# A two-layer hybrid decoder step: the sample tile of the mLSTM taken second, the second prompt tile last

## What is computed

```python
b = jnp.cumsum(lfc, axis=-1)
dmat = jnp.where(causal, b[..., :, None] - b[..., None, :] + lic[..., None, :], -jnp.inf)
inter = b + m[..., None]
m_t = jnp.maximum(inter, dmat.max(-1))
g_inter = jnp.exp(inter - m_t)
s = jnp.einsum('bhtd,bhsd->bhts', qc, kc) * jnp.exp(dmat - m_t[..., None])
num = g_inter[..., None] * jnp.einsum('bhtd,bhde->bhte', qc, C) + jnp.einsum('bhts,bhse->bhte', s, vc)
den = g_inter * jnp.einsum('bhtd,bhd->bht', qc, n) + s.sum(-1)
h = num / jnp.maximum(jnp.abs(den), jnp.exp(-m_t))[..., None]
...
C = dec[..., None, None] * C + jnp.einsum('bhs,bhsd,bhse->bhde', ws, kc, vc)
```

## Time and profile before

| what | us |
|---|---|
| median of 3 runs (lowest, highest) | 1525.32 (1524.56, 1529.46) |
| the profiled execution | 1525.5 |
| its span | 1523.7 |
| PE busy in the span | 1470.8 (97%) |
| DVE, ACT, POOL busy | 983.7, 696.0, 378.4 |
| growth multiply of step 14, 18, 26 starts, layer 0 | 420.86, 433.85, 456.96 |

### The profile page before, as it was taken

The page is one execution under the profiler, slowest core; times in us unless marked ns, Lnnn a source line. Parts: engine busy times, 40 slices in busy tenths (PEclk is TensorE's granted clock), DMA queues, the critical chain, the costliest instruction groups (busy, mean ns, idle before and its releaser), DMA issues.

```text
span 1523.7 us, 34030 instructions
## 1 busy us (share of the span) xinstructions
PE 1470.8 (97%) x13394; PEld 1415.6 (93%) x13394; DVE 983.7 (65%) x1579; ACT 696.0 (46%) x1188; POOL 378.4 (25%) x407
## 2 busy tenths in 40 slices
PE   7999999999988999999999999989999899999995
PEld 7999998899867999999999999979998689999995
DVE  4444435588475787775577776466874777877644
ACT  5333334766545543334443334366574455333332
POOL 4222362010531422220412222300124313222100
PEclk9999999999999999999999999999999999999998
DMA  8544543444113655544544545534521444555351
GB/s 220 151 145 146 166 152 83 132 121 122 33 40 112 172 152 151 151 138 152 158 132 144 151 152 157 151 90 124 131 74 31 122 116 138 160 151 170 126 166 35
DMA packets 318938, 198.82 MB, mean 130 GB/s; under 512 B 7792, under 2 KB 303760, under 8 KB 318832
## 3 DMA queue, kind: packets, MB, share of 16 engines
q1 hardware_dynamic: 315120, 190.69, 43.0%
q0 software_dynamic: 3712, 6.62, 2.2%
HBM read 188.50 MB, written 8.78 MB: 129 GB/s over the span
## 4 chain that ended last, share of the span: by engine, by line
PE 85%; DVE 8%; ACT 4%; issue 2%; DVEq 1%; DMA 0%; SPq 0%; ACTq 0%
PE bank L2113 24%; PE bank L2115 23%; PE bank L2114 23%; DVE wlo L2606 2%; PE bank L2200 1%; ACT whi L2403 1%; DVE raw L1571 1%; DVE rlo L2637 1%; PE bank L747 1%; ACT z L1176 1%; PE bank L2205 1%; PE bank L777 1%; PE bank L571 1%; PE bank L848 1%; PE bank L759 1%
## 5 line engine op out<-in xcount | busy, mean ns | idle before, releaser
L2403 ACT ACTIVATE whi<-raw 128x1024 fp32r<-128x1024 f32 x340 | 358.0, 1059 | 471.9 <-PE bank L2115 455.6
L2606 DVE TENSOR_TENSOR wlo<-raw,whi 128x1024 fp32r<-128x1024 f32 x340 | 421.4, 1243 | 228.7 <-ACT whi L2403 227.9
L2113 PE MATMUL bank<-rhi,whi 128*128 128x322 f32 x984 | 306.5, 311 | 0.0
L2115 PE MATMUL bank<-rhi,wlo 128*128 128x322 f32 x984 | 305.9, 311 | 0.0
L2114 PE MATMUL bank<-rlo,whi 128*128 128x322 f32 x984 | 304.9, 310 | 0.0
L2113 PE MATMUL bank<-xh,whi 128*128 128x320 f32 x912 | 284.9, 312 | 5.2 <-DVE xl L2780 3.2
L2114 PE MATMUL bank<-xl,whi 128*128 128x320 f32 x912 | 281.8, 309 | 0.0
L2115 PE MATMUL bank<-xh,wlo 128*128 128x320 f32 x912 | 281.8, 309 | 0.0
L2875 POOL TENSOR_TENSOR hl<-scratch,hh 128x320 f32 x88 | 146.9, 1669 | 494.9 <-DVE scratch L2727 379.6
L2113 PE MATMUL bank<-hh,whi 128*128 128x320 f32 (+1 forms) x704 | 218.4, 310 | 0.5 <-DVE wlo L2606 0.5
L2114 PE MATMUL bank<-hl,whi 128*128 128x320 f32 (+1 forms) x704 | 217.4, 309 | 0.0
(11 more groups left out here) (421 smaller groups left out, 1908.9 us busy)
## 6 DMA issues: line engine op xcount, KB each, us to landing
raw<-in_ffn_wg SPq DMA_DIRECT2D x88, 512.0 KB, 3.8
raw<-in_ffn_wu SPq DMA_DIRECT2D x88, 512.0 KB, 3.8
raw<-in_ffn_wd SPq DMA_DIRECT2D x88, 512.0 KB, 3.6
raw<-in_w_in SPq DMA_DIRECT2D x60, 512.0 KB, 3.8
raw<-in_w_out SPq DMA_DIRECT2D x16, 512.0 KB, 6.1
raw<-in_state_C SPq DMA_DIRECT2D x8, 512.0 KB, 6.1
out_s_C<-raw SPq DMA_DIRECT2D x8, 512.0 KB, 4.1
ring<-in_state_wkv POOLq DMA_DIRECT2D x8, 256.0 KB, 5.9
```

What stands on the lines that cost most here:

```text
L2113: pe.matmul(out, w_hi, hi, start=start, stop=False)
L2115: return pe.matmul(out, w_lo, hi, start=False, stop=stop)
L2403: act.activation(whi[:, slot, :], raw[:, slot, :], ACT.Copy).then_inc(hi_ready.sem, 1)
L2606: dve.tensor_tensor(wlo[:, slot, :], raw[:, slot, :], whi[:, slot, :].bitcast(F32), ALU.subtract).then_inc(lo_ready.sem, 1)
```

## The change

The sample becomes the second of the three tiles in time (`TURN`), and prompt tile 1 the last. The scores of the sample are now at step 9, its heads at steps 12 and 13, its C pieces at steps 14 to 17, two a step, its means, squares and spreads at steps 15 and 16. Prompt tile 1 has its scores at step 18, values at 21, memory added and means at 22, spreads at 23, scaling at 24, output products at 25. ACT's load of the table for the square root moves behind step 19. The exponential of the gate row goes to a buffer of its own for the sample (`rexp_s`).

`tile_scores` no longer spreads rows with `sel`. It transposes a column of `cols`, broadcast along the free axis. For this `gate_columns` turns five rows (four for tile 0), 14 products in place of 9, and `cols` has five columns.

On POOL the first `masked_values` goes to the front, `decay` waits only for the columns, and the first `memory_term` waits for the prompt's spreads (`hvar_ready` 2).

```diff
@@ gate_columns
-                for q in range(3):
-                    last = turn(pe, bank[4][0:rows, (n * 3 + q) * HB:(n * 3 + q + 1) * HB], row[:, q, at:at + rows])
+                for i, r in enumerate(COLUMNS):
+                    if n or i < 4:
+                        out = (n * 5 + i) * HB
+                        last = turn(pe, bank[4][0:rows, out:out + HB], row[:, r, at:at + rows])
@@ tile_scores
-                pe.wait_ge(num_ready.sem, num_ready.by(L, n))
-                pe.wait_ge(caug_ready.sem, caug_ready.by(L, n))
-            for r, b in ((5, 4), (6, 5)):
-                if n or r == 5:
+                pe.wait_ge(num_ready.sem, num_ready.by(L, TURN[n]))
+                pe.wait_ge(caug_ready.sem, caug_ready.by(L, 1))
+                if n == 1:
+                    pe.wait_ge(left_done.sem, left_done.by(L, 2 * HB))
+            for i, b in ((3, 4), (4, 5)):
+                if n or i == 3:
                     for h in range(HB):
-                        pe.matmul(bank[b][:, h * rows:(h + 1) * rows], sel[:, h, :], row[:, r, at:at + rows],
-                                  start=True, stop=True)
+                        pe.transpose(bank[b][:, h * rows:(h + 1) * rows],
+                                     cols[0:rows, n, i, h:h + 1].broadcast_to([rows, P]), ident[0:rows, 0:rows])
...
+        TURN = (0, 2, 1)
@@ tensor_mixers
-                    tile_scores(pe, L, 1 + SCORES_AT.index(n))
+                    tile_scores(pe, L, TURN[1 + SCORES_AT.index(n)])
...
-        LEFT = (("C", 0), ("C", 1), ("C", 2), ("C", 3), ("H", 0), ("H", 1), ("C", 4), ("C", 5), ("C", 6), ("C", 7),
-                ("H", 2), ("N", 0), ("T", 0))
+        LEFT = (*(("C", i) for i in range(2 * HB)), ("H", 2), ("H", 0), ("H", 1), ("N", 0), ("T", 0))
...
-        NUM_AT = (7, 12)
-        SCORES_AT = (9, 14)
-        HEAD_AT = (17, 18)
-        LEFT_AT = (20, 20, 21, 21, 22, 22, 23, 23, 24, 24, 25, 26, NSTEP)
+        NUM_AT = (7, 21)
+        SCORES_AT = (9, 18)
+        HEAD_AT = (12, 13)
+        LEFT_AT = (14, 14, 15, 15, 16, 16, 17, 17, 23, 25, 25, 26, NSTEP)
@@ scalar_mixers
-                if n == SQUARES_AT[0]:
+                if n == WEIGHTS_AT[2] + 1:
                     act.preload_act_table_set("sqrt_and_others")
...
-        WEIGHTS_AT = (4, 9, 14)
-        NUMS_OUT_AT = (7, 12, 19)
-        SQUARES_AT = (17, 20)
-        ROOTS_AT = (19, 22)
+        WEIGHTS_AT = (4, 9, 18)
+        NUMS_OUT_AT = (7, 13, 21)
+        SQUARES_AT = (15, 22)
+        ROOTS_AT = (20, 23)
@@ vector_mixers
-        LOGS_AT = (10, 15)
-        PRODUCTS_AT = (6, 11, 16)
-        ADDED_AT = (8, 13)
-        QUERIES_AT = 17
-        INTER_AT = 17
-        MEANS_AT = (17, 20)
-        SPREADS_AT = (19, 21)
-        SCALED_AT = (20, 23)
+        LOGS_AT = (10, 19)
+        PRODUCTS_AT = (6, 11, 20)
+        ADDED_AT = (8, 22)
+        QUERIES_AT = 12
+        INTER_AT = 13
+        MEANS_AT = (15, 22)
+        SPREADS_AT = (16, 23)
+        SCALED_AT = (21, 24)
@@ pool_mixers
+            masked_values(pool, L, 0)
             pool.memset(qm[:, :, :], 0.0).then_inc(qm_zero.sem, 1)
...
-            pool.wait_ge(tile_mm.sem, tile_mm.by(L, NTT))
+            pool.wait_ge(cols_turned.sem, cols_turned.by(L, 1))
...
-            pool.wait_ge(hvar_ready.sem, hvar_ready.by(L, 1))
+            pool.wait_ge(hvar_ready.sem, hvar_ready.by(L, 2))
             memory_term(pool, L, 1)
```

More of the change, by code:

```diff
@@ L195, in hymba_kernel @@
         gnst = area(3888, 2, NCH * NJ)
-        lim = area(3928, 32, rows=HB)
-        cols = area(3960, NTT, 3, HB)
-        small = area(4008, 96)
+        lim = area(3928, 24, rows=HB)
+        cols = area(3952, NTT, 5, HB)
+        small = area(4012, 88)
         n0 = area(4104, SB, HB)
@@ L259, in hymba_kernel @@
         hsq = area(0, 2 * HB * DK, of=spare)
-        vmask = [area(1536, SB, DK, of=spare), area(15304, SB, DK)]
+        vmask = [area(9480, SB, DK), area(15304, SB, DK)]
         s0 = area(12744, SB, NJ, NA)
@@ L516, in bonus_sums @@
             last.then_inc(rk_mm.sem, 1)
+        COLUMNS = (1, 2, 0, 5, 6)
         def gate_columns(pe, L):
@@ L645, in left_over @@
             elif kind == "H":
-                pe.wait_ge(h_ready.sem, h_ready.by(L, 1 if i < 2 else 2))
+                pe.wait_ge(h_ready.sem, h_ready.by(L, 2 if i < 2 else 1))
+                if i == 2:
+                    pe.wait_ge(caug_ready.sem, caug_ready.by(L, 2))
                 rows = TT[i][1]
@@ L1058, in copy_gate_columns @@
                 rows = TT[n][1]
-                src = bank[4][0:rows, n * 3 * HB:(n + 1) * 3 * HB].rearrange("p (q h) -> p q h", q=3)
-                act.activation(cols[0:rows, n, 0, :], src[:, 0, :], ACT.Copy)
-                last = act.activation(cols[0:rows, n, 1:3, :], src[:, 1:3, :], ACT.Exp)
-            last = act.activation(cols[PART[1], 2, 2, 0:HB:2], bank[4][PART[1], 8 * HB:9 * HB:2], ACT.Exp)
+                src = bank[4][0:rows, n * 5 * HB:(n + 1) * 5 * HB].rearrange("p (q h) -> p q h", q=5)
+                kept = 5 if n else 4
+                act.activation(cols[0:rows, n, 0:2, :], src[:, 0:2, :], ACT.Exp)
+                act.activation(cols[0:rows, n, 2:kept, :], src[:, 2:kept, :], ACT.Copy)
+            own = (2 * 5 + 1) * HB
+            last = act.activation(cols[PART[1], 2, 1, 0:HB:2], bank[4][PART[1], own:own + HB:2], ACT.Exp)
             last.then_inc(cols_ready.sem, 1)
@@ L1105, in tile_weights @@
             rows = TT[n][1]
-            act.wait_ge(tile_mm.sem, tile_mm.by(L, n + 1))
+            act.wait_ge(tile_mm.sem, tile_mm.by(L, TURN[n] + 1))
             if n:
-                act.activation(rexp[:, 0:HB * rows], bank[5][:, 0:HB * rows], ACT.Exp)
-            act.wait_ge(wlog_ready.sem, wlog_ready.by(L, n + 1))
+                act.activation((rexp if n == 1 else rexp_s)[:, 0:HB * rows], bank[5][:, 0:HB * rows], ACT.Exp)
+            act.wait_ge(wlog_ready.sem, wlog_ready.by(L, TURN[n] + 1))
             act.activation(wexp[0:rows, :, 0:rows], wexp[0:rows, :, 0:rows], ACT.Exp).then_inc(wexp_ready.sem, 1)
@@ L1570, in left_over_done @@
                     at = h * TS + s * ST + ST - 1
-                    last = dve.scalar_tensor_tensor(out=C0[:, h, s, :], in0=C0[:, h, s, :], scalar=rexp[:, at:at + 1],
+                    last = dve.scalar_tensor_tensor(out=C0[:, h, s, :], in0=C0[:, h, s, :], scalar=rexp_s[:, at:at + 1],
                                                     in1=b[:, k * DK:(k + 1) * DK], op0=ALU.mult, op1=ALU.add)
```

77 lines of the change are left out of this document (40 added, 37 removed).

## The result

The changed kernel takes 1544.69 us (median of 4 runs, 1544.19 to 1545.47), the kernel before 1525.04 beside it: a ratio of 1.0121, 95% interval 1.0106 to 1.0136. It is 1.2% slower, and above the range that was forecast, 1521 to 1535. The span of the profiled execution went from 1523.7 to 1543.1 us, by 19.4.

What follows compares the result with a forecast made beforehand. PE was taken to bound steps 5 to 14, DVE steps 18 to 26; per layer 0.9 - 2.5 + 2.5 + 2.8 = +3.7, for two +7.4, less 4.4 gives +3.0: 1528.3 us, range 1521 to 1535.

Steps and rivals of the forecast that it cites:

- the sum: Whole kernel: +3.7 us per layer, +7.4 for two, less 4.4, gives +3.0; forecast chance 0.48.
- steps 5 to 14: Growth front, bound by PE: sample replaces tile 1, -2.5 us per layer (-1.2 to -3.6); DVE's masked queries cost nothing.
- the clock: Slow stretch in front, 1.7 us: taken away there, none added in the tail, its gain left out of the -2.5.
- the recurrence: Stage behind the growth: both PE waits without a releaser go, -4.4 us for both layers; 0 if kept.
- PE's late instructions: Recurrence: PE's waits of 2.7 and 1.7 us, laid to w_out loads, vanish as these are issued inside the growth: -4.4.
- the tail runs at the lower clock: Rival, steps 18 to 26: one more slow stretch per layer gives 1531.7 us, two more 1535.1; chance 0.17.
- The gate columns: Ahead of step 5, PE-bound: five more turns cost +0.9 us per layer, bounds 0.6 and 1.1.
- Steps 14 to 18: Now bound by DVE with eight memory updates and a 2.3 us first wait: 15.5 us, +2.5 per layer (0 to +3.5).
- Steps 18 to 26: Tail, a chain of single pieces of the last tile: 25.9 us in place of 23.1, +2.8 per layer (0 to +5).
- the scaling beside POOL: Tail: DVE's scaling runs beside POOL's `memory_term`, 1.0 us added in steps 18 to 26.
- the tail is relieved: Rival: steps 18 to 26 stay at 23.1 us as DVE loses its updates; 1520.5 us, faster; chance 0.18.
- The rule on transposes: Skill's statement that transposes don't count as PE-busy the same way; by it they would bring slow stretches; left undecided.

Runs made afterwards that it cites:

- tuned: The changed kernel with POOL's decay behind the second masked values, memory terms waiting for the scaled outputs, five added PE products of 384 columns: 1531.78 us, ratio 1.0033.
- decay late: The changed kernel with POOL's `decay` put behind the second masked values: 1542.08 us, ratio to the kernel before 1.0098.

## Why the prediction was wrong

The forecast was 1528.3 us, with slower by more than 0.3% at 0.40, and the sign of the sum (+3.0) was right; its size was not. Two steps failed: a term that was put at nothing in steps 5 to 14, and the clock, which the sum held at its level of before, in the recurrence. The span grew by 16.4 us more than the sum had it; 8.2 of them lie in the recurrence of both layers, 5.5 in steps 5 to 14, 2.7 in the other three stages.

**Steps 5 to 14, the step that failed first.** The prediction wrote that logs, products and masked queries "cost nothing here, since DVE is idle for 15 of the 24 us", and that POOL's masked values and `decay`, moved ahead, "have nothing waiting for them". Both were true alone. Together they were not: the edit put `decay` and the queries beside each other, and queries beside a POOL instruction were the slow case of the earlier trace rows. The price named for it, 2 us, was that of one POOL instruction; here four follow each other, and two queries took 4.1, for which PE waited 3.2. With `decay` elsewhere the stage takes 21.2 and 22.0 us, so -3.1 and -1.8 in place of the -2.5 forecast. That this is near the forecast is partly luck: the slow stretch in front is gone as well, with which the prediction's bound was -3.6, and late instructions take 1.3 and 2.4 us of it, which the sum didn't have at this place. Without them the gain is some 4.3 us (estimated from these numbers), so PE's terms were too small. The Trainium skill, "SBUF — State Buffer", section "SBUF: two separate sides", says that DVE and GpSimd (POOL) share a pair of ports which is locked for a whole instruction, and the loser waits. The trace agrees, with the addition that the first query got no turn between three POOL instructions of about 1.0 us each, and the second waited out the fourth.

**The recurrence, the step that failed second.** The -4.4 for PE's late instructions was right in kind: in the changed kernel SP issues the loads from 454.24 on, they have landed by 463.7, ahead of step 26, and no wait of PE without a releaser is left in the recurrence.

```profile
454.24 4.31 SPq L2060 DMA_DIRECT2D raw<-in_w_out  x4
```

The changed kernel alone doesn't show why, since its clock was low there. But with added products in the tail the clock was high and the waits stayed away, and the run with late loads in the old order, and the one that puts them back into the recurrence, show the cause in both directions. What the sum lacked was the clock: by it this stage was to take 33.1 and 32.0 us; it took 36.3 and 36.9, and 30.2 where neither a slow stretch nor a late instruction fell into it (tuned, layer 0). The rival "the tail runs at the lower clock" named the clock rightly, with the wrong place and size: it counted one or two stretches of 3.4 us in steps 18 to 26, at 1.7 us each. One of 23.9 us came in each layer, most of it in the recurrence behind. It began right behind a window in which PE was busy for 1.4 of 3.4 us, and work put there made the recurrence 5 us shorter in each layer (36.3 and 36.9 to 31.4 and 31.7). But it is no property of the new order alone: the transposes in the old order had such a stretch in both layers of one execution, 20.5 and 17.1 us, the first of them with PE busy for 3.3 of the 3.4 us ahead of it. So idle time of PE is not needed for it; that it is the cause in the new order is likely, not shown. In the runs that were traced the changed order without added products had it in all six layers of three runs (23.9 and 23.9, 17.1 and 17.1, 17.1 and 23.9 us), with added products in the tail in one of eight, the old order in two of eight; work at the start of the recurrence had 10.2 us twice. Why it lasts once it has begun is not settled.

**What was right.** The gate columns cost 0.9 us; the further 1.1 in layer 1 are a slow stretch behind them at 1115.0, which the old order with its nine turns also had in one run (1104.2). Steps 14 to 18 were forecast at 15.5 us and took 16.0, with 2.6 us of first wait where 2.3 were taken. Steps 18 to 26 were forecast at 25.9 and took 26.5 and 26.2; of them 0.9 are the scaling beside POOL, where 1.0 was taken. The sum comes out near in part by luck: the clock was low for 8.0 and 7.4 us of this stage, and the prediction had balanced one stretch of 3.4 us there.

**What the sum hid.** It took the change as a whole, so that the transposes' gain and the order's loss stood in one term. Apart, in the profiled executions of layer 0, steps 5 to 26 take 60.4 us before, 57.2 with the transposes alone, and 66.9 with the new order. The order costs 9.7 us: 2.0 in the first part, 4.3 in steps 14 to 18, where the eight memory updates now stand in a stage that PE had filled (busy for 11.5 of 11.7 us with the transposes alone), and 3.3 in the tail. POOL's new order is part of this, since `decay` moved with it. The rival "the tail is relieved" fell: the tail lost its updates and still grew, as the last tile's pieces wait for each other.

**The rule on transposes.** The Trainium skill, "TensorE: Matmul & The Clock Gate", Part 4, would have transposes bring slow stretches. With the transposes in the old order the granted clock is 1.00 from step 5 to 18, where a slow stretch had been before. So it is in all four traced layers with transposes in the old order, while all four with `sel` products had a slow stretch of 3.4 or 6.8 us from about step 10 on. The runs do not bear it out at this place. That the same execution has a long slow stretch 25 us later, behind the growth, is not explained by them: with `sel` products the old order has the same instructions there.

## What to carry to other kernels

Where work is moved, lay the engines' new rows beside each other and look for pairs that share something, not only for queues: a piece that is free on DVE and a piece that is free on POOL can be dear together. Price parts of a change apart where they can stand alone; here one part was worth some -6 us (ratio 0.9958), and the rest of the change cost over 20 (by 1.0121 against 0.9958). Look at the clock behind a latency chain, not only in it: here a tail that left PE idle was followed in both layers by a stage of small products at the lower clock, which cost some 6 us there (36.3 us where 30.2 were seen without it), though such a stretch also came with next to no idle time ahead of it.

## What the runs showed of the hardware

- Once low, the granted clock stayed low for 17 to 24 us, with PE busy all the time in about half of it; before the change the same products had run at the higher level 3.4 us after it fell. Executions of one kernel differed by 10 us, with mean clocks of 0.987 and 0.976 (1536.5 and 1547.0).
- PE waited 0.7 to 3.2 us without a releaser, in 17 of 18 cases when large loads were under way: beside w_out in the recurrence, and beside or just behind the RWKV state at steps 11 to 13. All 18 ended 1.3 to 1.6 us behind the end of a 16-KB packet of the instruction queue. Where the clock was low such waits were not seen: the old order with transposes has none in the recurrence of either layer, with the loads of w_out beside it (458.6 to 469.7 and 1208.2 to 1219.0).
- DVE's multiply of 64 columns for one head took 0.21 us alone, and 3.10 and 3.42 in the two layers beside four POOL instructions in a row. The memory updates, which read one input from PSUM, took 2.16 us for eight beside the same four POOL instructions (decay late, 421.74), and 2.15 before the change.
